# Layer 0 cache pages loaded as 64 rows of 8 KB instead of 128 rows of 4 KB

## What is computed

```
past_a  = [(_gather_pages(cache_a_k[j], page_table), _gather_pages(cache_a_v[j], page_table)) ...]
k_all   = concatenate([past_k, k]);  v_all = concatenate([past_v, v])
s       = einsum('bqhcd,bkhcd->bhcqk', q, k_all) * HD_A ** -0.5
p       = softmax(where(k_pos <= q_pos, s, -inf))
a       = p[:, :, 0] - lam * p[:, :, 1]
o       = einsum('bhqk,bkhe->bqhe', a, v_all)
```

## Time and profile before

| what | us |
|---|---|
| median of three runs (1375.45 to 1377.22) | 1376.06 |
| the profiled execution, its own time | 1371.64 |
| its span, from the first to the last instruction | 1369.8 |
| layer 0's paged attention, from the first turned page to the last value product | 128.0 to 320.4 of the span |
| one sequence in that stage, from one `past_values` to the next | 23.6 |

### The profile page before, as it was taken

One profiled execution on the slowest core, in us unless ns is written; L12 is line 12 of the kernel. 1 busy time (PEld: TensorE's weight loads), 2 busy tenths in 40 slices (PEclk: granted clock), 3 DMA queues, 4 the chain that ended last, 5 costly groups with the idle time before them and its releaser, 6 DMA issues.

```text
span 1369.8 us, 18996 instructions
## 1 busy us (share of the span) xinstructions
PE 1193.8 (87%) x6635; PEld 602.1 (44%) x6636; DVE 475.4 (35%) x1035; ACT 337.6 (25%) x773; POOL 47.5 (3%) x81
## 2 busy tenths in 40 slices
PE   7998888887859999999589798898949999999856
PEld 3445666664433333333246445655433333333323
DVE  1012555552431111111444499366161111111263
ACT  1112444543011111211112414645011111211110
POOL 1200000000000000000100000000100000000100
PEclk9999999999959999999889999999958999999978
DMA  9935699979507799999541734334724979999721
GB/s 333 354 138 185 235 372 339 374 279 360 189 33 306 311 389 425 426 427 421 175 155 32 243 120 137 98 112 187 301 93 171 405 299 426 425 422 426 286 74 38
DMA packets 97278, 360.29 MB, mean 263 GB/s; under 512 B 17024, under 2 KB 35488, under 8 KB 75952
## 3 DMA queue, kind: packets, MB, share of 16 engines
q1 hardware_dynamic: 88528, 328.79, 61.6%
q0 software_dynamic: 5984, 21.59, 4.8%
q10 hardware_dynamic: 2688, 8.91, 1.7%
HBM read 341.48 MB, written 17.78 MB: 262 GB/s over the span
## 4 chain that ended last, share of the span: by engine, by line
PE 68%; DVE 10%; DMA 7%; SPq 5%; issue 5%; ACT 4%; DVEq 0%; POOL 0%; POOLq 0%; ACTq 0%
PE PS L871 15%; PE PS L597 13%; PE PS L892 7%; PE PS L844 6%; DMA ring<-in_moe_w_up 5%; PE PS L1019 4%; PE PS L1000 3%; PE PS L722 2%; PE PS L685 2%; PE PS L672 2%; SPq L360 2%; SPq L449 2%; PE PS L853 2%; PE PS L874 1%; PE PS L881 1%
## 5 line engine op out<-in xcount | busy, mean ns | idle before, releaser
L871 PE MATMUL PS<-ring,QKV 128*64 128x512 f32 (+1 forms) x512 | 231.2, 600 | 7.2 <-ACT QKV L1333 4.1
L874 PE MATMUL PS<-ring,QKV 128*64 128x512 f32 (+1 forms) x512 | 231.1, 600 | 0.0
L1333 ACT ACTIVATE QKV<-PS 128x512 f32<-128x512 f32 (+5 forms) x180 | 95.1, 528 | 399.2 <-PE PS L844 109.3
L597 PE MATMUL PS<-ring,XT 128*64 128x256 f32 (+1 forms) x576 | 150.6, 482 | 3.6 <-DMA ring<-in_a_w_in 2.9
L871 PEld LDWEIGHTS PS<-ring,QKV 128*64 128x64 f32 (+1 forms) x512 | 71.7, 142 | 153.1 <-issue 148.2
L892 PE MATMUL PS<-ring,QKV 128*64 128x512 f32 (+1 forms) x512 | 123.8, 598 | 0.0
L844 PE MATMUL PS<-X,QKV 128*64 128x512 f32 x432 | 103.6, 615 | 15.1 <-issue 15.1
L597 PEld LDWEIGHTS PS<-ring,XT 128*64 128x64 f32 (+1 forms) x576 | 71.1, 162 | 83.1 <-issue 73.0
L2004 DVE TENSOR_TENSOR QKV<-QKV,PS 64x512 f32<-64x512 f32 (+1 forms) x32 | 21.8, 680 | 233.8 <-ACT QKV L1508 233.8
L2009 DVE COPY QKV<-PS 64x512 f32<-64x512 f32 (+1 forms) x32 | 22.2, 693 | 189.1 <-PE PS L892 189.1
L1000 PE MATMUL PS<-ring,XT 128*128 128x512 f32 (+1 forms) x256 | 75.3, 509 | 7.7 <-ACT XT L1333 7.7
(11 more groups left out here) (311 smaller groups left out, 1304.5 us busy)
## 6 DMA issues: line engine op xcount, KB each, us to landing
ring<-in_moe_w_gate SPq DMA_DIRECT2D x32, 2048.0 KB, 12.1
ring<-in_moe_w_up SPq DMA_DIRECT2D x32, 2048.0 KB, 16.2
ring<-in_moe_w_down SPq DMA_DIRECT2D x32, 2048.0 KB, 14.1
ring<-in_cache_a_k SPq DMA_DIRECT2D x64, 512.0 KB, 6.0
ring<-in_cache_a_v SPq DMA_DIRECT2D x64, 512.0 KB, 5.7
ring<-in_a_w_in SPq DMA_DIRECT2D x5, 2048.0 KB, 25.5
ring<-in_ple_gate_w SPq DMA_DIRECT2D x4, 2048.0 KB, 13.2
ring<-in_cache_b_k SPq DMA_DIRECT2D x64, 128.0 KB, 2.0
```

The costliest lines, as they stand in the source:

```text
L597: ins = pe.matmul(PS[p0:p1, banks[u % 4], 0:c1 - c0], rows_of(k, t), wt[:, k, c0:c1], start=(k == 0), stop=(k == KD - 1))
L871: ins = pe.matmul(PS[0:m, 0, :], XE[:, k, 0:m], wg[:, k, :], start=(k == 0), stop=(k == KD - 1))
L874: ins = pe.matmul(PS[p1:p1 + m, 1, :], XE[:, k, 0:m], wu[:, k, :], start=(k == 0), stop=(k == KD - 1))
L1333: ins = act.activation(dst, src, ACT.Copy) if scale is None else \
```

## The change

A page is now loaded as 64 rows of 8 KB: two neighbouring keys, which are contiguous in memory, go to one partition. Page `j` takes partitions 0 to 63 if `j` is even and 64 to 127 if it is odd, and the column blocks of both pages of the pair. So a pair of pages fills the same 128 partitions x 8 KB as before, but which key lies where is different: a block of 128 rows that is turned by one `page_turn` now has 64 keys of either page. Keys and values are laid out alike, so the products over keys still match.

Since a turned block has keys of both pages of a pair, the key semaphores are now one to a pair, and `page_turn` of either half of the pair waits for both pages. No instruction is added, removed or put in another place on any engine. The number of DMAs (128 in this stage) and the bytes of each (512 KB) stay, and so do SP's waits.

```diff
-        k_landed = [S(f"kpage_landed{s}") for s in range(NPAGE)]
+        k_landed = [S(f"kpages_landed{s}") for s in range(NPAGE // 2)]
...
+            def half_pages(pages, j):
+                q, h = j // 2, j % 2
+                return pages[64 * h:64 * h + 64, 2 * q:2 * q + 2, :].rearrange("p j n -> p (j n)")
+
             def key_page(b, j):
...
-                sp.dma_start(kpage[:, j, :], cache_a_k[0, bass.ds(pg, 1)].rearrange("a p h d -> (a p) (h d)"))\
-                  .then_inc(k_landed[j], 16)
+                sp.dma_start(half_pages(kpage, j), cache_a_k[0, bass.ds(pg, 1)].rearrange("a (p u) h d -> (a p) (u h d)", u=2))\
+                  .then_inc(k_landed[j // 2], 16)
...
-                sp.dma_start(vpage[:, (b % 2) * NPAGE + j, :],
-                             cache_a_v[0, bass.ds(pg, 1)].rearrange("a p h d -> (a p) (h d)"))\
+                sp.dma_start(half_pages(vpage, (b % 2) * NPAGE + j),
+                             cache_a_v[0, bass.ds(pg, 1)].rearrange("a (p u) h d -> (a p) (u h d)", u=2))\
                   .then_inc(v_landed[b % 2], 16)
...
-                pe.wait_ge(k_landed[j], b * 16 + 16)
+                pe.wait_ge(k_landed[j // 2], b * 32 + 32)
```

## The result

The changed kernel takes 1462.99 us, the median of 4 runs (1460.77 to 1466.42), beside 1376.64 us for the kernel before on the same chip (4 runs, 1375.45 to 1377.70): a ratio of 1.0636, with a 95% interval of 1.061 to 1.0663. The change makes the kernel 86 us slower. The profiled execution of the changed kernel took 1460.77 us, 1459.0 of them its span.

The account below looks back on a forecast made before the run. The prediction took computing, 23.6 us a sequence in layer 0's paged attention, as the bound, with transfers 16% away. Pages at 2.37 us add 80 us, other terms 0: 1376 + 80 = 1456 us, range 1373 to 1472.

Parts of the forecast that it names:

- What bounds the stage: Layer 0's paged attention: computing sets 23.6 us a sequence; transfers decide once a page takes more than 1.475 us.
- 8 KB rows are worth nothing: Page loads: longer rows make a page 1.245 us, freeing 2.4 us of DMA engines that nobody waits for.
- 64 partitions at 2.37 us a page: Page loads: half the partitions move at a lone store's 221 GB/s, so transfers set the stage's time, adding 80 us.
- The landing of the last pair at 385.2, and nothing else behind it: Sequence 7's key pages 6 and 7 land at 385.2 instead of page 6's turn at 304.9; later work only shifts.
- The pair's wait at 0: PE's wait for both key pages of a pair: taken as 0, between 0 and 5 us over six sequences.
- halves side by side: Rival for page loads: opposite halves are written at once, the 23.6 us period stays, 1376 us; chance 0.18.
- the row of zeros at 396 GB/s: Filling `places` from 32 partitions at a time on POOL's queue, cited as evidence that partial-partition transfers need not be slow.
- Partly in step: Rival for page loads: engines stray and share a half part of the time, 1.8 us a page, 1403 us; chance 0.20.
- PE's clock: Rival in the page stage: PE's clock falls to 0.50 and PE becomes the bound, 1499 us; chance 0.02.
- the bound at 0.61: Page stage: at clock 0.61 PE needs 37 us a sequence, still under the transfers' 38, so they hide it.
- The signs: Expected profile: DMA share about 1.0, 210 to 240 GB/s, 38 us a sequence, waits mostly on pages 2 and 6.
- 64 partitions instead of 128: Page loads: the number of partitions one DMA reaches was the disputed price, 1.245 to 2.37 us a page.

Follow-up runs that it names:

- (g) of the first set: Kernel before with page loads alone behind its last product: two pages in one load, 128 rows of 8 KB to all partitions; 418 to 426 GB/s.
- (b): Kernel before with page loads alone behind its last product: 64 rows of 8 KB, always to partitions 0 to 63; 212 to 222 GB/s.

## Why the prediction was right, and by how much it was off

*What bounds the stage.* Right. The later of the two, 23.6 us of computing or the pages of a sequence, set the time on both sides: 16 pages at 2.4 us did, over the threshold of 1.475 us a page; 8 pages of the same kind, and 16 pages at some 1.25 us (every second partition), left the time of before.

*8 KB rows are worth nothing.* Right: 1.000 with full partitions, 1.0008 with every second one. Where the queue was full the size was right too: with every second partition 426 GB/s from 170 to 182 us make a page 1.23 us, against 1.245 in the prediction. Over a whole sequence of that kernel the share of the DMA engines is 0.94, beside 0.93 before, so not even the engines were freed there.

*64 partitions at 2.37 us a page.* The transfers set the stage's time as forecast, and the term was a little too small. From the first value page of sequence 2 (issued at 158.57) to the turn of page 6 of sequence 7, less 2.1 us of landing, a page took (390.84 - 2.1 - 158.57) / 94 = 2.45 us. Over 94 pages the 0.08 us are 7.5 us; the stage began 1.8 us earlier in this execution (154.35 against 156.12 in the earlier trace rows), so the turn was late by 86.0 us instead of 80.3. The rate of the long stretch, 217 GB/s, makes 2.42 us, and 2.43 without the 0.20 of its 47.64 MB that are instructions and not pages; the remaining 0.02 us a page, 2 us in all, weren't traced. The price came from a single store of 1.4 us, 221 GB/s, and alternating loads measured alone have the same 221. The change's own pattern, two pages to a half, has 214, or 2.45 us. That a store's rate would hold for loads was assumed, and nothing in the kernel before showed it. It holds for one half alone (stores 218, loads 212) and fails for halves in turn (stores 305, loads 221). So the size came out in part by luck: the price was taken from a kind of store that behaves as loads do.

*The landing of the last pair at 385.2, and nothing else behind it.* The first is 390.84 by the working above. Behind it, 3.2 us more were lost that the prediction had at zero. Some 2 of them are seen in PE's work at the lower clock (1.6 us in the last value products, 0.4 in the last scores, 2.30 against 1.92); the rest wasn't traced. So the spans differ by 89.2 us and the medians by 86.4, where the prediction had 80.

*The pair's wait at 0.* Right: ratio 1.0006, one wait of 1.1 us in the profile, within its bounds of 0 to 5 us.

*The rival "halves side by side".* It fell: 217 GB/s at a share of 1.02, and the halves in turn, which favour it most, gained 4% by themselves and 1% of the kernel's time. The step that misled here was the row of zeros at 396 GB/s as evidence for it. It was a series of stores on POOL's queue, and stores from several parts of SBUF do get to 343 GB/s, where loads don't. It was given 0.18. The rate of several stores together said nothing of loads. "Partly in step" has a grain of truth only with the halves in turn, 242 GB/s at the stage's end.

*The rival "PE's clock".* The granted clock fell to 0.81, not to 0.50; PE was busy 65% of the stage, so the transfers hid it, as the bound at 0.61 said. In the timeline the eight transposes behind three of the five waits shown take 1.97 us, not 1.09: from 196.5 to 198.5 us, after the wait of 5.07 us, the granted clock was 0.50 (1.2 GHz), and from 390.8 to 391.9 us, after that of 3.98, it was 1.00 (2.4 GHz). The length of the wait alone doesn't decide it: from 236.1 to 238.1 us, after 3.77, it was 0.50.

*The signs.* The DMA share is 1.02 at 217 GB/s, the page-6 turns of sequence 2 and 3 lie 39.6 us apart (196.52, 236.08), pages land after 17.8 us, and the long waits are on pages 2 and 6. Not foreseen were the shorter ones on page 0, such as the 2.13 us at 206.37.

*The step that was wrong in its words.* "64 partitions instead of 128" was named as the cause. The number of partitions is not the cause: every second partition, or 32 to 95, cost nothing. The time came out, because each load of the change stays on one side of the border between 63 and 64.

## What to carry to other kernels

Before a load is rearranged, work out its threshold: the time of the computing over the number of transfers, against bytes over the rate. A load that must leave partitions free should take every second partition or a range that lies evenly across the border at 64, such as 32 to 95, not the lower or the upper half; in this kernel the choice of every second partition instead of a half was worth 6% by itself. When a price has to be taken from a row of the other direction, say that it is an assumption and measure it: here a lone store had the price of the loads, and stores in turn had not.

## What the runs showed of the hardware

- The DMA share doesn't show this cost. Loads at 212 and at 426 GB/s both keep the 16 engines at a share of 1.01 to 1.04; only the GB/s beside it tell that each packet takes twice as long. In the trace's records a packet of 8 KB took 309 ns by the median in (g) of the first set and 641 in (b).
- Loads to halves in turn hardly overlap (221 GB/s; 242 at most, after some 160 us of such loads), loads on two queues to opposite halves reach 245, stores in turn 305, and stores of quarters 259 (SP's queue) and 343 (POOL's). The Trainium skill, "SBUF — State Buffer", section "Can I just issue two DMAs to hit both halves?", has +6% for two concurrent transfers; the 4% of loads in turn agree, the 16% of loads on two queues (245 against 212) and the 40% of stores in turn (305 against 218) go beyond it. Why stores get apart and loads don't was not settled.
- SP's time to issue a page depends on the shape of the load: 0.33 us by the median for 128 rows of 4 KB, 0.47 for 64 rows of 8 KB, to a half or to every second partition, and 0.60 for two rows of 4 KB to each of 64 partitions. The 128 rows of 8 KB of a 1 MB load took 0.39, so it isn't the length of the rows; what it is was not settled. In the kernel after (all key pages from 156 to 400 us: ns min/median/max, first and last start):

```profile
L385 SPq DMA_DIRECT2D ring<-in_cache_a_k x47: 468/468/942, 159.8 to 366.2; - x47
```

  With a page every 2.4 us, or every 1.475 us, it costs nothing here: the kernel with every second partition issues as slowly and has the time of before.
